# Two transformer blocks on one core: the residual kept transposed, the norm factor applied to the products, stationary weights nearly everywhere

## What is computed

```python
# block 1: layer 0 with differential attention, layer 1 with neighbourhood attention
for i in range(2):
    h = h + mix_i(rmsnorm(h, norm_mix[i]))                    # qkv, attention, w_o
    h = h + (silu(n @ w_gate[i]) * (n @ w_up[i])) @ w_down[i] # n = rmsnorm(h, norm_ffn[i])
    h = h + sigmoid(rmsnorm(h, norm_ple[i]) @ ple_w_gate[i]) * (p[i] @ ple_w_proj[i])
h = rmsnorm(h, norm_final)
# block 2: layer 0 with convolution and pooling ("ev"), layer 1 with two attentions
for i in range(2):
    h = h + mixer_i(rmsnorm(h, mix_norm_g_2[i]))
    z = rmsnorm(h, ffn_norm_g_2[i]) @ ffn_w_in_2[i];  u, g = split(z)
    a = causal_dwconv(u, conv_w, 3 taps) + conv_b
    h = h + (silu(a) * g) @ ffn_w_out_2[i]
return rmsnorm(h, final_norm_g_2)

def rmsnorm(x, g): return x * rsqrt(mean(x * x, over the features) + 1e-6) * g
```

## Time and profile before

| | |
|---|---|
| median of 3 runs | 1384.99 us (1384.25 to 1385.16) |
| the profiled execution | 1385.34 us |
| its span in the profile | 1383.5 us (1.8 us lie around it) |
| TensorE matmul busy | 1327.9 us, 96% |
| VectorE busy | 810.0 us, 59% |
| ScalarE busy | 639.7 us, 48% |
| GpSimd busy | 110.4 us, 8% |
| granted TensorE clock | 0.99 of full speed |

### The profile page before, as it was taken

How to read it: one execution, slowest core, us unless ns; L and a number is a source line. 1 busy time by engine, 2 the same in 40 slices (tenths; PEclk the granted TensorE clock), 3 DMA queues, 4 the chain that set the end, 5 groups by cost and what they waited for, 6 DMA issues and landing times.

```text
span 1383.5 us, 21886 instructions
## 1 busy us (share of the span) xinstructions
PE 1327.9 (96%) x8658; PEld 1183.8 (86%) x8658; DVE 810.0 (59%) x989; ACT 639.7 (46%) x917; POOL 110.4 (8%) x137
## 2 busy tenths in 40 slices
PE   6999989999999999999998998999999999999998
PEld 5987879988778768999886988999878887899986
DVE  5686465544656565555446566667547456666653
ACT  4465344443545544444334444455434444555532
POOL 2001170000100000000000601300002000000000
PEclk9999999999999999999999999999999999999999
DMA  9523686655544236665554656866646423566551
GB/s 336 174 99 104 144 226 182 182 192 194 184 137 153 92 93 165 182 183 184 182 182 137 207 163 194 218 193 191 213 152 191 130 92 94 144 178 181 186 192 59
DMA packets 246401, 231.18 MB, mean 167 GB/s; under 512 B 7080, under 2 KB 221264, under 8 KB 246208
## 3 DMA queue, kind: packets, MB, share of 16 engines
q1 hardware_dynamic: 242656, 215.57, 50.8%
q0 software_dynamic: 3680, 14.70, 3.6%
HBM read 229.18 MB, written 2.63 MB: 168 GB/s over the span
## 4 chain that ended last, share of the span: by engine, by line
PE 88%; DVE 4%; ACT 2%; DMA 2%; POOL 2%; issue 1%; SPq 0%; DVEq 0%; POOLq 0%; ACTq 0%
PE bank L1250 16%; PE bank L1251 16%; PE bank L1252 16%; PE bank L1287 10%; PE bank L1290 9%; PE bank L1293 9%; PE bank L1358 3%; PE bank L1218 2%; PE bank L1404 2%; DMA raw<-in_ffn_w_up 1%; ACT bank L548 1%; PE bank L1378 1%; DVE wlo L819 1%; PE bank L1282 1%; PE bank L1280 1%
## 5 line engine op out<-in xcount | busy, mean ns | idle before, releaser
L819 DVE TENSOR_TENSOR wlo<-raw,whi 128x2048 fp32r<-128x2048 f32 x203 | 471.6, 2326 | 305.6 <-ACT whi L531 305.4
L1250 PE MATMUL bank<-xhi,whi 128*128 128x256 f32 x1880 | 539.0, 287 | 6.7 <-DVE wlo L819 6.7
L1251 PE MATMUL bank<-xlo,whi 128*128 128x256 f32 x1880 | 532.6, 283 | 0.0
L1252 PE MATMUL bank<-xhi,wlo 128*128 128x256 f32 x1880 | 532.4, 283 | 0.0
L531 ACT CAST whi<-raw 128x2048 fp32r<-128x2048 f32 x203 | 385.6, 1901 | 198.4 <-PE bank L1293 167.7
L1250 PEld LDWEIGHTS bank<-xhi,whi 128*128 128x128 f32 x1880 | 361.2, 192 | 16.3 <-issue 7.4
L1251 PEld LDWEIGHTS bank<-xlo,whi 128*128 128x128 f32 x1880 | 361.4, 192 | 0.2
L1252 PEld LDWEIGHTS bank<-xhi,wlo 128*128 128x128 f32 x1880 | 361.2, 192 | 0.0
L1287 PE MATMUL bank<-whi,hidhi 128*128 128x512 f32 x336 | 105.9, 396 | 0.0
L1290 PE MATMUL bank<-wlo,hidhi 128*128 128x512 f32 x336 | 105.8, 395 | 0.0
L1293 PE MATMUL bank<-whi,hidlo 128*128 128x512 f32 x336 | 105.8, 395 | 0.0
(11 more groups left out here) (173 smaller groups left out, 1342.0 us busy)
## 6 DMA issues: line engine op xcount, KB each, us to landing
raw<-in_ffn_w_in SPq DMA_DIRECT2D x88, 512.0 KB, 5.0
raw<-in_ffn_w_gate SPq DMA_DIRECT2D x44, 512.0 KB, 4.0
raw<-in_ffn_w_up SPq DMA_DIRECT2D x44, 512.0 KB, 5.2
raw<-in_ffn_w_down SPq DMA_DIRECT2D x44, 512.0 KB, 4.4
raw<-in_ffn_w_out SPq DMA_DIRECT2D x44, 512.0 KB, 4.4
raw<-in_da_w_qkv SPq DMA_DIRECT2D x24, 512.0 KB, 5.4
raw<-in_na_w_qkv SPq DMA_DIRECT2D x24, 512.0 KB, 4.4
raw<-in_od_w_in SPq DMA_DIRECT2D x24, 512.0 KB, 4.5
```

The source lines that it names most:

```text
L819: nc.vector.tensor_tensor(wlo[:, c % RING, :], raw[:, c % RING, :], whi[:, c % RING, :].bitcast(F32), ALU.subtract).then_inc(w_lo, 1)
L1250: mm(dst, hi[:, k, cs], xhi[:, k, :], start=(k == 0), stop=False)
L1251: mm(dst, hi[:, k, cs], xlo[:, k, :], start=False, stop=False)
L1252: ins = mm(dst, lo[:, k, cs], xhi[:, k, :], start=False, stop=(k == KT - 1))
```

## The change

- **Layout.** `x` comes in transposed by the host, `h` is kept with features on the partitions, and the output is transposed back by the host. The 320 matmuls with a diagonal and the copies after them are gone.
- **Norm.** The product is made of `h` times the gain alone (`take_x` on ScalarE, `lo_x` on VectorE). The sum of squares now runs over partitions: ScalarE squares pairs of feature tiles, GpSimd adds the four pairs (`add_squares`, three additions of 128x512), TensorE sums over the partitions with a vector of ones (`sum_squares`, 4 matmuls), GpSimd takes the power, VectorE builds diagonals, TensorE spreads the factor to all partitions (`spread_r`, 2 matmuls), VectorE copies it (`rst`). The factor is multiplied onto the *results* of the product by VectorE, which so takes over what ScalarE read from PSUM in qk and ev.
- **Chunks.** wo, proj, evout become kind G and gate kind F: weights stationary, 48 matmuls of 256 columns where there were 24 of 512. down becomes kind D: 256 output features at a time, 12 chunks in place of 11, the third of each group smaller. v stays as it was.
- **512-column products.** In ffn0, ffn1 and all down stages high and low input lie side by side, so that one matmul of 512 columns does high weight by both, and one of 256 does low weight by high input (`two`): 16 of each kind in a chunk. The two halves of the bank are added up afterwards by VectorE.
- **Feed-forward loops.** In layers 0 and 1 ScalarE copies the second halves out of PSUM, VectorE adds the first halves, then multiplies by the factor, then ScalarE does the silu. In layers 2 and 3 VectorE multiplies by the factor from PSUM to SBUF before ScalarE's first tap.
- The gate's sigmoid, f3 (now after v3) and the constants are moved to fit.

The core of the diff:

```diff
@@ ScalarE, ffn, body of a chunk @@
-                    ac.wait_ge(w_used, c0 + 1 + j)
...
-                        nc.scalar.activation(act[:, jj, :], b[:, 0:S], ACT.Identity,
...
-                        nc.scalar.activation(act[:, jj, :], b[:, 0:S], ACT.Silu
...
                     if conv:
+                        ac.wait_ge(gu_ok, base + 1 + j)
...
+                        nc.scalar.activation(acc[:, jj, :], gu[:, jj, 0, :], ACT.Identity,
...
+                        hi_before()
+                    else:
+                        b0 = FFN_BANKS[layer][jj][0]
+                        ac.wait_ge(w_used, c0 + 1 + j)
+                        nc.scalar.copy(gu[:, jj, :, :], ps[:, b0:b0 + 2, S:2 * S]
+                                       ).then_inc(part_ok, 1)
+                        hi_before()
+                        ac.wait_ge(gu_ok, base + 1 + j)
+                        nc.scalar.activation(gu[:, jj, 0, :], gu[:, jj, 0, :], ACT.Silu
...
                     if conv:
                         ac.wait_ge(conv_ok, FT * (layer - 2) + 1 + j)
...
                     split(c0 + jj + RING, turn)
@@ VectorE, ffn, body of a chunk @@
                     if conv:
+                        ve.wait_ge(w_used, c0 + 1 + j)
...
+                        b = bank(FFN_BANKS[layer][jj]).rearrange("p (f t) -> p f t", f=2)
+                        nc.vector.tensor_tensor(g, b, over2(rst[:]), ALU.mult).then_inc(gu_ok, 1)
+                        lo_before(turn, jj, first)
...
+                        ve.wait_ge(conv_a, n)
...
+                        split(c0 + jj + RING, turn)
+                        ve.wait_ge(silu_ok, base + 1 + j)
+                        nc.vector.tensor_tensor(a, a, gu[:, jj, 1, :], ALU.mult
+                                                ).then_inc(mul_ok, 1)
+                        return
...
+                    ve.wait_ge(part_ok, n)
+                    nc.vector.tensor_tensor(g, ps[:, b0:b0 + 2, 0:S], g, ALU.add
+                                            ).then_inc(sum_ok, 1)
+                    ve.wait_ge(sum_ok, n)
+                    nc.vector.tensor_tensor(g, g, over2(rst[:]), ALU.mult).then_inc(gu_ok, 1)
+                    lo_before(turn, jj, first)
...
@@ TensorE @@
-            def norm(name, t):
-
-                pe.wait_ge(hn_ok, 2 * XNORM[name] + t + 1)
...
+            def sum_squares(name):
+
+                n = NORM[name]
+                pe.wait_ge(add_ok, add_base(n + 1))
...
+            def spread_r(name):
+
+                n = NORM[name]
+                pe.wait_ge(diag_ok, n + 1)
...
+            def two(dst, hi, lo, x, start, stop):
+
...
+                mm(dst, hi, x.rearrange("p a t -> p (a t)"), start=start, stop=False)
+                return mm(dst[:, 0:S], lo, x[:, 0, :], start=False, stop=False)
...
+            def ffn(layer):
...
+                    middle = (lambda: spread_r(name)) if first and jj == 1 else None
@@ VectorE, the gate @@
+                    nc.vector.tensor_tensor(gu[:, i % RING, :, :], src, over2(rst[:]), ALU.mult
+                                            ).then_inc(g_raw, 1)
+                    ve.wait_ge(g_sig, 4 * layer + i + 1)
...
+                    nc.vector.tensor_tensor(hpair(i), gu_gate(i), hpair(i), ALU.add
+                                            ).then_inc(h_ok, 1)
+                    split(START[gate] + i + RING)
+                    lo_x(target, i)
```

1415 lines of the change are left out of this document (825 added, 590 removed).

## The result

The changed kernel takes 1512.7 us (median of 4 runs, 1506.8 to 1518.4) against 1384.7 (1384.3 to 1385.2) for the kernel before: a ratio of 1.0926, 95% interval 1.0897 to 1.0954. The profiled execution took 1512.1 us, its span is 1510.3 us. I had forecast 1442, with 1466 as the upper end.

What follows compares the result with a forecast made beforehand. The prediction took TensorE's columns to bound the kernel; its stage terms, mainly +43 and +44.6 us for the conv stages, summed to +57.2 on 1385.3: 1442 us, 4% slower. Its own range was 1418 to 1462, the 8-in-10 range 1405 to 1466.

Steps and rivals of the forecast that it cites:

- The conv loops: ffn2 and ffn3 with their downs: 8.01 us a body against TensorE's 5.75, 239 us a stage, +43 and +44.6 us.
- The ring: VectorE and ScalarE waiting on each other in layers 2 and 3: 5.60 us a body before, 8.01 after the change.
- E: End of the product before a conv stage; VectorE's first body was to start at E+11, its split end at E+19.2.
- ffn0, ffn1, projection and gate 0: Layer 0 feed-forward -2.2 us, layer 1 +0.7, at 6.0 us a body; proj, gate and mix norm -15.6.
- The three attentions: VectorE's 8 copies of 0.69 us each lie under TensorE; +0.6 us in all.
- Projection 1 to evout: proj, gate and mix norm of layer 1 -11.1 us with 5.6 of waiting; ev and evout +0.9.
- Start and end: Start -2 us, an estimate; end +5.1 us, 11.7 against 6.6.
- v3 to wo3: down2 to v3 falls from 32.8 to 26 us, -6.8, with a share of the attentions' +0.6.
- Rings don't bind: Rival for the conv stages and ffn0, ffn1: every wait hidden, 117 us less, 1325 us; chance 0.10.
- The ring is shorter: Rival: high and low part (0.84 us) or more fall out of the conv ring, 1400 us; chance 0.08.
- GpSimd gets in the way: Rival: its additions slow VectorE's splits at the norms; with hand-overs at their upper bound 1465 to 1475 us; chance 0.10.
- The clock falls: Rival: half the 44 conv chunks at 1.2 GHz, 11.5 us each, +77, 1519 us; chance 0.03.

Runs made afterwards that it cites:

- a1: Changed kernel with VectorE's copies of q and k moved earlier in its order, ahead of the normalisation and the probabilities': 1499.4 us, ratio 1.0832.
- c1: Changed kernel with ScalarE's weight copy ahead of the silu and the high part ahead of the first tap in layers 2 and 3: 1403.6 us, ratio 1.0142.
- b0: Changed kernel with conv-loop product and split later, q and k copies and ScalarE's bias earlier, output projection begun in other banks: 1390.9 us, ratio 1.0054.
- p1: Changed kernel with GpSimd's additions of squares cut from 512 to 2 columns, so the numbers differ from the reference: 1501.2 us, ratio 1.0847.
- b3: b0 with squares' additions on VectorE and further reordering in ffn0, ffn1, the gate loops and behind the output projections: 1363.0 us, ratio 0.9835.
- f1: Changed kernel with 12 more unread 256-column matmuls per chunk in the loops of layers 2 and 3, from the second chunk: 1513.5 us, ratio 1.0926.
- n1: b3 with 12 more unread one-column products (24 instructions) on TensorE ahead of 8 of its 11 sums of squares: 1388.5 us, ratio 1.0028.

## Why the prediction was wrong

Direction, place and mechanism of the main loss were right; the total was 70 us short. Two steps failed, the attentions (28 us) and the way from projection 1 to evout (16), and the conv loops were sized 18 us short. The start, the end and v3 to wo3 add 9, and the other stages give back 1.5. Measured stretches against the earlier trace rows and the terms of the sum:

- **The conv loops: right, sizes 18 us short.** +43 and +44.6 forecast, +52.8 and +52.9 measured. The ring has the links of the prediction; 8.28 us instead of 8.01, the hand-over from the multiplication to ScalarE's tap taking 0.92 and not 0.73, and the high part back to VectorE 0.56 and not 0.44. That is 0.27 x 42 = 11 us over both stages. The rest is not the end: from the end of the last body's split to the last product of down2 and down3 it took 51.3 and 52.8 us, for 51.9 in the forecast. It is the beginning, since the first body's split ended at E+21.2 in both stages (E as in the prediction) for my E+19.2, and one body of ffn2, which took 11.1 us for 8.3. There GpSimd works on `t5b`, and a tap takes 1.23 us where it takes 0.48 above; that the one makes the other is read from the trace and no run removes it:

```profile
891.39 9.64 POOL L581 TENSOR_TENSOR t5b<-t5b,cst 128x384 f32<-128x384 f32 x8 [8.18 <-DMA t5b<-t_scratch]
...
896.83 1.23 DVE L1192 SCALAR_TENSOR_TENSOR acc<-gu,col,acc 128x255 f32<-128x255 f32 x1
```

  The multiplication between them, which reads one input from PSUM, keeps its 0.68 us.
- **ffn0, ffn1, projection and gate 0: right.** -3.1 for -2.2 and -0.6 for +0.7; splits 5.90 us apart for the 6.0 forecast; -14.9 for -15.6, with no gap on TensorE between gate0 and v1 (30.20 of 30.20 us busy), as I had said. But in this last one I set the whole old stretch against a new one that holds nothing of v1, where 18 of v1's 96 products had stood in the old one: 4.1 us of my gain was only a border.
- **The three attentions: this step failed.** I wrote that VectorE's copies "lie under TensorE; wo's finer waits give 1 to 2 us, its columns cost 1.6: +0.6 in all". Between first score and last product with v they cost 16.1 + 4.6 + 1.7 = 22.4 us. By whole stages, up to the end of wo0 and wo1, the first two cost +16.5 and +11.9, of which 4.1 are the border named above. I asked how long a copy takes and whether VectorE had room, and not what is queued ahead of it: a1 gets 15.2 of the 16.1 back by the place of the copies alone (10.5 against c1's execution), b0 a further 2.9 of attention 1 by the place of ScalarE's bias and by the banks, though most of it only moved ahead of the first score.
- **Projection 1 to evout: this step failed too.** -10.2 forecast, +5.4 measured. The last two of the gate's bodies took 8.2 us for my 6.5, by the additions beside the low parts, and the clock stood at 0.90. TensorE waited 8.2 us in ev's first chunk, for my 5.6. I had the collision as a rival, at the norms' splits, and did not look where else the additions lie. p1 gives back 5.7 of the 15.6 us; b3, which moves the additions to VectorE and changes the order of the gate's body as well, 12.3. Which part of the rest is order and which is clock stays open.
- **Start and end:** +0.7 for -2, +7.5 for +5.1. v3 to wo3: -2.3 for -6.8 and attention 2's share of the +0.6.
- **Rivals.** *Rings don't bind*: excluded by c1, and by the trace's 62% of VectorE beside 64 us of waiting for it; occupancy, the measure named there, said nothing on the order. *The ring is shorter*: excluded, since high and low part stand in the ring of 8.28 us. *GpSimd gets in the way*: true as a part, 5.7 us at the gate by p1. *The clock falls*: it fell in the loops, one of my own signs of being wrong, and was free there (f1); it cost in attention 0. I had priced it in the wrong place, and too high: at n1's pitch of 0.21 us a conv chunk of 48 products takes 10.3 us at half clock, not 11.5. I had also read the clock from the stretches with idle time and passed over the first row, with 11.6 us idle of 39.5 at 1.00. My own range of 1418 to 1462 counted the 10 us for the stages between at its lower end only; at the upper end they make it 1473, still short. No rival had the attentions in it, and the range ended where the forecast's own mechanism ended; each stage between the loops had an error of its own, and nearly all had the same sign.
